# A written-out instruction order for a two-layer decoder step: when the planner puts a group of expert dots, a gelu or a weight transpose ahead of the next stage

## The reference

```
x = x + mixer(rmsnorm(x))            # w_in 1024x2568, mLSTM heads + pooling, w_out 1024x1024
xn = rmsnorm(x)
q  = xn @ peer_wq                    # 1024 x 2048
s  = q . sub_keys                    # 8 heads, 2 halves, 128 keys each
top 16 of each half -> 256 sums -> top 16 of those -> eidx (16 experts a head, 128 a token)
gate = softmax(top)
act  = gelu(sum_d xn[t,d] * u_tab[eidx[t,k], d])      # 128 dots of width 1024 a token
x = x + sum_k gate*act * v_tab[eidx[t,k], :]          # 128 rows of width 1024 a token
x = x + sigmoid(x @ w_gate) * (p @ w_ple)
```

## Time and profile before

| | |
|---|---|
| median of 3 runs | 1942.24 us |
| the profiled execution, its time | 1939.56 us |
| its span, first to last instruction | 1937.8 us |
| TensorE busy / VectorE busy / GpSimd busy | 1034.4 / 1095.3 / 1156.0 us |
| bytes moved by DMA | 687.24 MB, of them 553.72 MB by the gathers' queue |
| load and store of the sample state, once a layer each | 2064.0 KB |
| mean DMA rate over the span | 355 GB/s |
| mean granted TensorE clock | 0.762 of full speed |

### The profile page before, as it was taken

The page is one execution under the profiler, slowest core; times in us unless marked ns, Lnnn a source line. Parts: engine busy times, 40 slices in busy tenths (PEclk is TensorE's granted clock), DMA queues, the critical chain, the costliest instruction groups (busy, mean ns, idle before and its releaser), DMA issues.

```text
span 1937.8 us, 18049 instructions
## 1 busy us (share of the span) xinstructions
PE 1034.4 (53%) x6274; PEld 477.3 (25%) x6274; DVE 1095.3 (57%) x2851; ACT 173.9 (9%) x297; POOL 1156.0 (60%) x1062
## 2 busy tenths in 40 slices
PE   7867230574754654717655766465854640035556
PEld 3433120332311232304111333332311120021113
DVE  1266898867920467888800486968950179960001
ACT  2222010000100011100000022101100010000001
POOL 0033556254677766676677767456576787777770
PEclk9888665687878876758778978777876675568888
DMA  7577767697999999999999999899799999999993
GB/s 294 190 297 283 260 223 283 181 380 294 385 409 409 409 413 412 372 377 353 410 409 409 405 407 408 275 359 399 256 401 410 409 404 409 409 409 409 409 409 144
DMA packets 173192, 687.24 MB, mean 355 GB/s; under 512 B 19856, under 2 KB 21520, under 8 KB 158366
## 3 DMA queue, kind: packets, MB, share of 16 engines
q0 software_dynamic: 152064, 553.72, 73.1%
q1 hardware_dynamic: 21038, 132.37, 18.0%
HBM read 679.88 MB, written 6.59 MB: 354 GB/s over the span
## 4 chain that ended last, share of the span: by engine, by line
DMA 32%; POOL 24%; PE 17%; DVE 15%; issue 11%; ACT 1%; SPq 0%; DVEq 0%; ACTq 0%; POOLq 0%
POOL rows L1182 24%; DMA rows<-in_v,index_tb 10%; DMA rows<-in_u,index_A 7%; PE bank L728 7%; DMA rows<-in_v,index_ta 7%; PE acc L1010 6%; DMA rows<-in_u,index_B 4%; DVE rows L1747 4%; DMA wring<-in_w 1%; DVE scratch L1570 1%; DMA rows<-in_v,index_S 1%; DVE scratch L1644 1%; PE bank L725 1%; DVE scratch L1694 1%; DVE scratch L1693 1%
## 5 line engine op out<-in xcount | busy, mean ns | idle before, releaser
L1182 POOL DMA_INDIRECT rows<-in_u,index_A x256 | 325.3, 1271 | 365.6 <-DVE index_A L1722 178.4
L1010 PE MATMUL acc<-rows,wz 128*32 128x512 f32 x2048 | 341.4, 798 | 289.2 <-DMA rows<-in_v,index_tb 142.8
L728 PE MATMUL bank<-wring,turned 128*128 128x512 f32 x832 | 410.3, 645 | 69.9 <-DVE decayed L1454 33.0
L1182 POOL DMA_INDIRECT rows<-in_u,index_B x256 | 299.8, 1171 | 108.8 <-issue 71.0
L1747 DVE SCALAR_TENSOR_TENSOR rows<-rows,xn_a 128x1024 f32<-128x1024 f32 x256 | 304.7, 1224 | 79.9 <-DMA rows<-in_u,index_A 76.6
L1182 POOL DMA_INDIRECT rows<-in_v,index_ta x256 | 252.6, 987 | 145.0 <-PE acc L1010 78.2
L1747 DVE SCALAR_TENSOR_TENSOR rows<-rows,xn_b 128x1024 f32<-128x1024 f32 x256 | 306.9, 1226 | 56.7 <-DMA rows<-in_u,index_B 51.1
L1182 POOL DMA_INDIRECT rows<-in_v,index_tb x256 | 242.3, 946 | 107.7 <-issue 61.9
L728 PEld LDWEIGHTS bank<-wring,turned 128*128 128x128 f32 x832 | 165.6, 208 | 272.5 <-issue 245.9
L1010 PEld LDWEIGHTS acc<-rows,wz 128*32 128x32 f32 x2048 | 74.0, 127 | 532.9 <-issue 510.7
L1780 DVE TENSOR_TENSOR x_b<-x_b,acc 128x1024 f32<-128x1024 f32 x2 | 2.4, 1222 | 260.6 <-PE acc L1010 260.6
(11 more groups left out here) (293 smaller groups left out, 997.5 us busy)
## 6 DMA issues: line engine op xcount, KB each, us to landing
wring<-in_w SPq DMA_DIRECT2D x108, 1024.0 KB, 8.1
scratch<-in_c_s SPq DMA_DIRECT2D x2, 2064.0 KB, 11.1
out_c_s<-scratch SPq DMA_DIRECT2D x2, 2064.0 KB, 9.9
rows<-in_u,index_A POOLq DMA_INDIRECT x256, 11.4
rows<-in_v,index_ta POOLq DMA_INDIRECT x256, 7.7
rows<-in_u,index_B POOLq DMA_INDIRECT x256, 9.2
rows<-in_v,index_tb POOLq DMA_INDIRECT x256, 7.9
keys<-in_keys SPq DMA_DIRECT2D x2, 1024.0 KB, 9.8
```

Of the source, the lines that this page charges most:

```text
L728: ins = pe.matmul(ps[:, :], turned["A"][:, 4 * h + c, :], w[:, c, :], start=first, stop=end, skip_group_check=True)
L1010: ins = pe.matmul(acc[i * QUAD:(i + 1) * QUAD, c, :], wz[:, i, g * QUAD:(g + 1) * QUAD], row, start=first, stop=end, skip_group_check=True)
L1182: pool.indirect_dma_start(out=rows[:, n % RING, :], out_offset=None, in_=a[table], in_offset=bass.IndirectOffsetOnAxis(ap=which[:, at:at + ...
```

## The change

Three branches are put ahead of the rule of choice, and a constant. `Clocks.run` returns, as a third value, the time that the asked entry would hold the counted engines (its steps on them and the idle time).

```diff
+MARGIN = 6.0
@@ Clocks.run
         if not for_real:
-            return idle, start if start is not None else now
+            held = sum(us for engine, us in self.steps(e) if engine in engines)
+            return idle, start if start is not None else now, held + idle
@@ woven
-    groups, stages, waited = list(groups), list(stages), 0
+    groups, stages, waited, half_done = list(groups), list(stages), 0, set()
     def emit(e):
         clocks.run(e, True)
         out.append(e)
+        if e[0] in ("project", "mix", "query", "gate"):
+            half_done.symmetric_difference_update([(e[0], e[2], e[4])])
@@ the choice, where both sides can go
+        elif half_done and groups[0][0] == "dots" and KIND[groups[0][1]] == "S":
+            take = "stage"
+        elif groups[0][0] in ("gelu", "weights", "add"):
+            take = "group" if of_group[1] <= of_stage[1] + 0.5 else "stage"
+        elif blocked == "slot" and of_group[0] <= 0.3 and of_group[1] + of_stage[2] > clocks.dma - MARGIN:
+            take = "group"
         elif stages[0][0] in RANKING and blocked != "index":
```

## The result

The changed kernel takes 1920.54 us (median of 4, 1918.42 to 1921.14) against 1941.33 (1937.94 to 1944.46) in the same session: a ratio of 0.9889, interval 0.987 to 0.9908. It gains 21 us; the forecast was 47, at 1895. Both stretches that the forecast named came down, and others gave part of it back.

What follows compares the result with a forecast made beforehand. Bound by DMA at 409 GB/s where it runs full, elsewhere by what keeps gathers from being issued. 78.7 + 3 won, less 28 bursts, 4 stores, 3 joints, is 46.7 us: 1895 us, own range 1880 to 1908, wider range 1862 to 1922.

Steps and rivals of the forecast that it cites:

- Both stretches that the forecast named: 350 to 400 and 1350 to 1410: 20.7 and 20.5 us lost, which a better order can win.
- The bursts: Dots back to back from 348 and near 1215 slow gather issue: 14 us each, 28 in all, bounds 0 to 50.
- The free bursts rival: VectorE soon row-bound and POOL issuing as in 1600 to 1700: the 28 us come back, 1867 us; chance 0.14.
- The state store: Store of the sample state in a full queue: 2 us each beyond its bytes, 4 for both.
- The joints: From the end of each dots burst to wz and the first vals: 3 us for all, 0 to 10.
- burst 1: First weave from 348, dry start, 44 dots in one burst, 32 rows to be moved: cost 14 us.
- Two signs that the prediction had named: No POOL wait over 10 us on dots or vals after 348; wrong if vals fall under 400 GB/s from stages holding TensorE.
- The rival of late indices: Postponed stages wait behind vals in TensorE's list, so indices of tiles 1 and 4 come late: 1984 us; chance 0.08.
- The second weave: Gelu branch puts tile 1's weights ahead: 3 us counted as won of the 4.6 lost in 895 to 920.
- Only the gelu branch: Third branch hardly fires or its dots are taken back by later stages: 37 us left, 1905 us; chance 0.1.
- Heavy bursts: Both bursts at 279 GB/s: they cost 50 us in place of 28, time 1917 us; chance 0.15.

Runs made afterwards that it cites:

- e2: Changed kernel without its second branch, so weights wait behind ranking or sample stages as under the old rule: 1909.65 us, ratio 0.9864.
- f1: Changed kernel run again unedited, xn in SBUF, on the chip of f2, f3 and f4: 1914.62 us, ratio 0.9886.
- f2: Changed kernel with dots that read xn from PSUM, as base for f3 and f4: 1873.73 us, ratio 0.9667.
- e9: Changed kernel with dots that read xn from PSUM, where the kernel before takes 1934.3 us: 1872.79 us, ratio 0.9673.
- f3: f2 with the store of the sample state cut from 2064 to 64 KB in both layers: 1863.25 us, ratio 0.962.
- f4: f2 with a margin of 12 in place of 6 for vals groups alone, so they go ahead of dense stages sooner: 1881.71 us, ratio 0.9721.
- e11: Kernel before, old order, with dots that read xn from PSUM: 1915.93 us, ratio 0.9902.
- e1: Changed kernel without its third branch (blocked on "slot"), so no dots are brought ahead of sample stages: 1924.83 us, ratio 0.9923.
- e12: Changed kernel without the gelu, weights and add branch, with dots that read xn from PSUM: 1875.89 us, ratio 0.9684.
- e3: Changed kernel once more, unedited, on the chip of e1 and e2: 1915.76 us, ratio 0.9891.
- g1: f2's kernel with the store of m (128 rows of 4 bytes) cut to one row in both layers, on another chip: 2031.66 us, ratio 0.9856.
- g2: f2's kernel with the store of the samples' u_in (128 rows of 512 bytes) cut to one row in both layers, on g1's chip: 2045.81 us, ratio 0.9928.
- e6: Changed kernel with dots that read xn from PSUM, on a chip where the kernel before took 2034.17 us: 2032.6 us, ratio 0.9995.
- e8: Changed kernel with the store of the sample state cut from 2064 to 64 KB per layer, on e6's chip: 2007.79 us, ratio 0.9879.

## Why the prediction was half right

**The order did what was said.** The dots stand in two blocks, no gather waits on a dot or a sample_write in 350 to 400, product to wz is 1 us, the last pass is nearly unchanged (31.8 us lost from gather 792 on before, 33.5 after). The first u_B gather came at 623.36, forecast 621. Taking dots first is right, and e2 shows that it is the branch that pays.

**The bursts were priced right.** Forecast 28 us for both. f1 loses 11.1 and 19.2 us in gathers 96 to 128 and 560 to 664, f2 0.6 and 3.3: 30 us, 26 of them contention. The split is worse than the sum: 14 and 14 were forecast, 11 and 19 came. The whole price of contention, f1 less f2, is 41 us, and the kernel before pays 18 of it too (1934.3 less 1915.93), so 22 fall to the change in the times. The free bursts rival, chance 0.14, was wrong with xn in SBUF and describes e9 nearly (1867 forecast, 1872.79 measured). By the Trainium skill's inference (SBUF — State Buffer, "Who interferes with whom") writing descriptors isn't delayed by a VectorE operation with two SBUF inputs; the runs show gathers 1.5 us in the median in place of 0.94 and up to 1.99, and 41 us. Its other rule, that a VectorE instruction with one SBUF input leaves GpSimd alone, agrees with the PSUM runs here (0.94 us).

**The state store was mis-sized,** and misnamed: 2 us a layer forecast on top of its bytes, 0 measured for it (f3) but 5.5 for the m store behind it. In the kernel before these 5.5 us lay where the DMA had little to do, which I read as the big store's price, with 7.5 as its bound. The step cost 11 us in place of 4: 7 us of the gap.

**The joints were mis-sized,** and the vals after them had no price. "I give 3 us for all such joints (0 to 10)." In the ledger gathers 128 to 160 and 664 to 792 lose 14.2 + 13.7 us in the changed kernel and 10.6 + 13.7 in f1; less 11 for the m stores that is 13 to 17. wz is in time, but vals groups stand in TensorE's list among the postponed stages, and I had looked at the chain from dots to wz, not at what comes after wz. Two places show it. Behind burst 1, in 410:432, the first three vals groups (L1020) share TensorE with the sample stages (L866), and gather 148 waits 5.9 us for the third:

```profile
L1020 PE MATMUL acc<-rows,wz 128*32 128x512 f32 x48 | 8.5, 848 | 4.1 <-DMA rows<-in_v,index_ta 4.1
L866 PE MATMUL bank<-mixer,qk 128*128 128x258 f32 x30 | 8.1, 399 | 0.3 <-DVE scratch L1580 0.2
```

In the second layer the joint itself cost nothing (408 and 405 GB/s in 1300:1310 and 1310:1320). The loss is 80 gathers on, at gather 736: in 1436:1456 TensorE is busy 12.93 of 20 us, VectorE 18.44, POOL waits 7.7 us in one piece, the rate is 257, and match (L940, L946) stands between vals groups:

```profile
1436.08 1.93 PE L1020 MATMUL acc<-rows,wz 128*32 128x512 f32 x16
1437.93 1.16 PE L940 MATMUL bank<-keys,q_t 128*128 128x128 f32 x8
1438.93 3.74 PE L946 MATMUL bank<-keys,mixer 128*128 128x128 f32 x32
1442.59 3.64 PE L1020 MATMUL acc<-rows,wz 128*32 128x512 f32 x32
```

In f4, which moved vals ahead, POOL's wait in 400:440 fell to 3.4 us, but the loss came up behind it, and the second layer got worse. So the loss is measured; that vals behind stages make all of it is read from the traces and not shown. Two signs that the prediction had named came true here: a wait of over 10 us on a vals group (14.3, right behind the m store) and a rate under 400 GB/s in vals (257). The rival of late indices had this mechanism, TensorE's order among vals, but turned round: I let stages wait for vals, and vals waited for stages. Another 10 to 14 us of the gap.

**The second weave** was to win 3 us and lost 6: 9 of the gap. In e9 against e11 (no contention) 256 to 528 still loses 3.3 us more, so the order itself costs there. e1 has the loss too (19.4), where of the two only the gelu branch is in. Cut at gather 384 the column has two parts. Gathers 384 to 528 lose 6.5 to 7.2 us in all four orders without the gelu branch (before, e2, e11, e12) and 7.7 to 10.3 in those with it: the branch that was to win 3 us there costs some 2. Gathers 256 to 384 lose 6.8 before and 8.0 to 12.1 after (e1, e2, e3, f1 and the first run), but 1.1 to 2.2 in every order with xn in PSUM: more of the contention of dots and gathers, in a stretch where the forecast had none.

**The sum again, for f1.** Bursts 2 us over the forecast, stores 7, joints and vals 10, second weave 10 make 29; its ledger (22.9, 20.7 and 32.6) has 29.7 over the forecast in the three middle columns. Against them stand 8.9 us won ahead of gather 96 (132.6 less 48.8 + 24.9 + 50.0), with 1.8 lost after gather 792: 46.7 - 29.7 + 8.9 - 1.8 = 24.1, and the spans differ by 1937.8 - 1913.7 = 24.1. The 8.9 (3 and 9 in the two other executions) I can't explain: the two orders are the same up to dots group 42, which frees the slot of gather 96. With one trace of the kernel before it may be scatter, and then the change is worth less by it.

**The rivals.** Only the gelu branch was forecast at 37 us of gain, 15.4 + 20.5 of it before the first vals; alone it has 14. In e1 gathers 128 to 160 lose 3.5 us in place of 15.3, as forecast, but 664 to 792 still lose 13.0 of 20.4, and 256 to 528 take 5.6 back. Late indices stayed away: 31 us to spare at tile 1, 50 at tile 4 (1470.6 against 1521.0). Heavy bursts has the time nearest to the measured one, 1917, but by luck: the bursts ran at 314 and 320 GB/s, not at 279, and cost 30 us, not 50.

## What to carry to other kernels

A stall that is scheduled away brings up what stood in its shadow: here the issue of gathers beside dots, a small store, and vals groups among the stages that had been postponed; price these before the gain. Ask of each VectorE operation in a gathering stretch whether its second operand can stand in PSUM: that one edit was worth twice the change of order, and doubled what the order brings, on the chips where the kernel before takes 1934 to 1941 us. When the DMA share is 1.0 and the rate half, look at packet sizes, not at bytes.

## What the hardware showed that I had not expected

- A store of 128 rows of 4 bytes took the DMA of all queues from 409 to about 185 GB/s for 10 us (g1 without it: 424); 128 rows of 512 bytes did nothing measurable (g1 has them, g2 hasn't), and 2 MB in rows of 16.5 KB cost 10.5 us for both layers, its bytes.
- Chips differ. The kernel before took 1934 to 1941 us in four sessions and 2034 and 2059 on two other chips. There the vals of the last pass ran at 364 to 369 GB/s, while the dots ahead of them reach 410, as slices 33 to 38 of e6's page show:

```profile
GB/s 299 184 290 290 351 229 173 410 223 404 378 341 362 410 414 380 410 289 399 379 371 347 348 351 380 315 320 361 371 298 381 409 301 410 410 320 369 364 367 121
```

- On such a chip the change and the PSUM edit together brought nothing (0.9995), and the edit alone made the order before 1.3% slower, though the gathers in the burst were as short as elsewhere. e8, the changed kernel with xn in SBUF and without the big store, was 25 us under e6 there, and the store's bytes are only 10 of them (an estimate from f3): so the edit seems to cost some 15 us with the changed order too. Why a gain of 60 us vanishes there stays open; the changed kernel itself was not run on these chips. Time the edit on more than one.
